# Head copies behind each weight chunk, and index sums in one block: a two-model transformer kernel on one core

## What is computed

```python
h = rmsnorm(x, norm_g)
proj = h @ w_in                     # 1024 -> queries, keys, values, gates
ya = moba_attention(rope(a_q), rope(a_k), a_v)            # 6 heads
# sparse attention "dsa": scores of 4 index heads choose 64 keys for each query
logit = einsum(iq, ik)
idx_score = sum over 4 index heads of relu(logit) * iw
idx_score = where(key <= query, idx_score, -inf)
sel = top_k(idx_score, 64)
yb = attention(rope(b_q), rope(b_k), b_v) over the chosen keys   # 6 heads
yc = dilated_mixture(rope(c_q), rope(c_k), c_v)            # 12 heads
merged = sum of sigmoid gates * (y @ w_branch);  x + merged @ w_out
```

## Time and profile before

| | before |
|---|---|
| median of 3 executions | 2262.8 us |
| the profiled execution, its own time | 2264.01 us |
| its span | 2262.2 us |
| its mean granted TensorE clock | 0.996 of full |
| PE busy | 2205.5 us, 97% |
| POOL, DVE, ACT busy | 1341.6, 1062.3, 837.1 us |
| data moved by DMA | 356.38 MB, mean 158 GB/s |

### The profile page before, as it was taken

The page is one execution under the profiler, slowest core; times in us unless marked ns, Lnnn a source line. Parts: engine busy times, 40 slices in busy tenths (PEclk is TensorE's granted clock), DMA queues, the critical chain, the costliest instruction groups (busy, mean ns, idle before and its releaser), DMA issues.

```text
span 2262.2 us, 38755 instructions
## 1 busy us (share of the span) xinstructions
PE 2205.5 (97%) x13484; PEld 1966.9 (87%) x13484; DVE 1062.3 (47%) x2066; ACT 837.1 (37%) x1294; POOL 1341.6 (59%) x704
## 2 busy tenths in 40 slices
PE   8889998899999999999999999999999999999999
PEld 8889998889988888888888888888888988999999
DVE  7664466654665544267555422655522511233323
ACT  5355553554532222244222222422222413665444
POOL 6664786648765554423555444555544644558997
PEclk9999999999999999999999999999999999999999
DMA  8942468624455543312555432555533423325555
GB/s 300 250 152 101 149 242 253 200 86 141 149 214 194 201 160 92 105 62 104 212 185 190 143 108 89 201 197 187 196 89 96 163 103 102 104 77 178 188 181 158
DMA packets 111378, 356.38 MB, mean 158 GB/s; under 512 B 12200, under 2 KB 20904, under 8 KB 110896
## 3 DMA queue, kind: packets, MB, share of 16 engines
q1 hardware_dynamic: 111280, 355.07, 47.1%
HBM read 347.40 MB, written 1.05 MB: 154 GB/s over the span
## 4 chain that ended last, share of the span: by engine, by line
PE 80%; POOL 6%; DVE 6%; issue 4%; DMA 2%; ACT 1%; SPq 1%; POOLq 0%; DVEq 0%; ACTq 0%
PE ps L2086 21%; PE ps L2087 21%; PE ps L2088 21%; POOL w_low L1161 5%; PE ps L2135 2%; PE ps L2136 2%; PE ps L2137 2%; DMA raw<-in_wv_dram 1%; PE ps L2591 1%; PE ps L2257 1%; PE ps L2225 1%; DVE ps L1406 1%; PE ps L2098 1%; DVE idx L1528 1%; PE ps L2290 1%
## 5 line engine op out<-in xcount | busy, mean ns | idle before, releaser
L1161 POOL TENSOR_TENSOR w_low<-raw,w_high 128x1024 fp32r<-128x1024 f32 (+3 forms) x542 | 1200.3, 2224 | 662.4 <-ACT w_high L624 661.6
L624 ACT ACTIVATE w_high<-raw 128x1024 fp32r<-128x1024 f32 (+3 forms) x544 | 537.0, 989 | 1084.8 <-PE ps L2088 844.1
L2086 PE MATMUL ps<-h_high,w_high 128*128 128x256 f32 (+2 forms) x2408 | 804.3, 334 | 21.7 <-POOL w_low L1161 12.5
L2087 PE MATMUL ps<-h_low,w_high 128*128 128x256 f32 (+2 forms) x2408 | 794.5, 330 | 0.0
L2088 PE MATMUL ps<-h_high,w_low 128*128 128x256 f32 (+2 forms) x2408 | 794.4, 330 | 0.0
L2086 PEld LDWEIGHTS ps<-h_high,w_high 128*128 128x128 f32 x2408 | 455.9, 189 | 68.1 <-issue 16.9
L2088 PEld LDWEIGHTS ps<-h_high,w_low 128*128 128x128 f32 x2408 | 457.0, 190 | 42.3
L2087 PEld LDWEIGHTS ps<-h_low,w_high 128*128 128x128 f32 x2408 | 456.2, 189 | 42.8
L2086 PE MATMUL ps<-act_high,w_high 128*128 128x256 f32 (+1 forms) x1058 | 345.6, 327 | 1.5 <-DVE act_low L2022 1.5
L2087 PE MATMUL ps<-act_low,w_high 128*128 128x256 f32 (+1 forms) x1058 | 344.7, 326 | 0.0
L2088 PE MATMUL ps<-act_high,w_low 128*128 128x256 f32 (+1 forms) x1058 | 344.7, 326 | 0.0
(11 more groups left out here) (251 smaller groups left out, 2236.2 us busy)
## 6 DMA issues: line engine op xcount, KB each, us to landing
raw<-in_w_dram SPq DMA_DIRECT2D x216, 512.0 KB, 3.3
raw<-in_wu_dram SPq DMA_DIRECT2D x176, 512.0 KB, 4.1
ada<-in_ada_dram SPq DMA_DIRECT2D x144, 512.0 KB, 3.3
raw<-in_wd_dram SPq DMA_DIRECT2D x64, 384.0 KB, 3.1
raw<-in_wd_dram SPq DMA_DIRECT2D x64, 320.0 KB, 2.9
raw<-in_wv_dram SPq DMA_DIRECT2D x24, 408.0 KB, 5.1
heads<-rot SPq DMA_DIRECT2D x16, 256.0 KB, 9.3
ada<-in_cond_dram SPq DMA_DIRECT2D x6, 512.0 KB, 5.2
```

The lines of the kernel that those rows point to most:

```text
L624: e.activation(wh[:, c % RING, at_:at_ + w], raw[:, c % RING, 0:w], ACT.Copy).then_inc(hi_done, 1)
L1161: e.tensor_tensor(wl[:, c % RING, at_:at_ + w], raw[:, c % RING, 0:w], wh[:, c % RING, at_:at_ + w].bitcast(F32), ALU.subtract).then_inc(l ...
L2086: e.matmul(ps[:, bank, to:to + n], wh[:, j, w], hi, start=(first and t == tiles[0]), stop=False)
L2087: e.matmul(ps[:, bank, to:to + n], wh[:, j, w], low, start=False, stop=False)
```

## The change

**Heads.** The copies are cut smaller: each group of four heads has 8 copies of 64 KB (32 rows, 2 tiles, 256 columns), two for each quarter of the partitions. Behind the load of chunk c (counted through qk and vn) two of them are issued, for group (c-13) // 4 and quarter (c-13) % 4, from chunk 13 on; they wait until the four chunks of their own group are rotated. The last two and the four of 32 KB come behind the last vn chunk's load, ahead of the first mix chunk's. A layer has 52 copies instead of 20, with the same bytes. PE waits for all of them at the same place.

**Index sums.** `index_step` becomes `index_scores(qt)`, all five operations in a row, called right ahead of the first top-k round of each half: in unit 0 (behind the maxima of units 0 and 1 and the gates 0 to 2) and in unit 8 (behind the maxima of 8 and 9 and the division of unit 7). The last sum has a semaphore of its own, `idx_summed`.

```diff
-            def heads_of(d0, g, n, parts):
-                e.wait_ge(emptied_d, 4 + d0 + RING * (g + n))
+            def heads_of(d0, g, parts=range(4)):
+                e.wait_ge(emptied_d, 4 + d0 + RING * g + RING)
                 for jq in parts:
                     for r in range(2):
                         dst = 64 * (jq % 2) + 32 * r
-                        e.dma_start(head_tiles[dst:dst + 32, 2 * g:2 * g + 2 * n, jq // 2, :],
-                                    rot_tiles[32 * jq:32 * jq + 32, 2 * g:2 * g + 2 * n, r, :]).then_inc(heads_in, 16)
+                        e.dma_start(head_tiles[dst:dst + 32, bass.ds(2 * g, 2), jq // 2, :],
+                                    rot_tiles[32 * jq:32 * jq + 32, bass.ds(2 * g, 2), r, :]).then_inc(heads_in, 16)
+
+            def heads_behind(d0, c):
+                c -= 3 * RING + 1
+                if c >= 0:
+                    heads_of(d0, c // RING, (c % RING,))
...
                         if j % 2 and i > 1:
                             ada_row(r0 + 2 * (i - 1) + j // 2, j // 2)
-                        if i == QK // RING - 1:
-                            heads_of(d0, 0, 4, (j,))
+                        heads_behind(d0, RING * i + j)
...
                         if i == 0 and j % 2:
                             ada_row(r0 + ADA_L - 2 + j // 2, j // 2)
-                        if i == 2 and j < 2:
-                            heads_of(d0, 4, 2, (2 * j, 2 * j + 1))
-                        if i == 2 and j == 2:
-                            for jq, half in ((2, 1), (3, 0)):
...
+                        heads_behind(d0, QK + RING * i + j)
+                heads_behind(d0, QK + VN)
+                for jq, half in ((2, 1), (3, 0)):
+                    for r in range(2):
+                        dst = 64 * half + 32 * r
+                        e.dma_start(heads[dst:dst + 32, NPOS // 2, :],
+                                    rot[32 * jq:32 * jq + 32, QK - 2 + r, :]).then_inc(heads_in, 16)
                 load(m1 + VN, 2 * RING, W8, w1_d, w0 + QK)
...
-                def index_step(qt, h):
+                def index_scores(qt):
                     w = P * (qt + 1)
                     acc = idx[:, qt, 0:w]
...
+                    e.wait_ge(relu_done, n_relu())
+                    e.tensor_scalar(acc, relu[qt][:, 0, 0:w], iw[:, qt, 0:1], None, ALU.mult).then_inc(dve_step, 1)
+                    own(1)
+                    for h in range(1, 4):
+                        last = e.scalar_tensor_tensor(out=acc, in0=relu[qt][:, 2 * (h % 2) + h // 2, 0:w], scalar=iw[:, qt, h:h + 1],
+                                                      in1=acc, op0=ALU.mult, op1=ALU.add)
+                        if h < 3:
+                            last.then_inc(dve_step, 1)
+                            own(1)
+                    last.then_inc(idx_summed, 1)
+                    e.wait_ge(idx_summed, n_relu.now)
+                    e.tensor_tensor(idx[:, qt, w - P:w], idx[:, qt, w - P:w], tri, ALU.add).then_inc(dve_step, 1)
+                    own(1)
...
                 n_nsplit(2 * KT)
-                for h in range(5):
-                    index_step(0, h)
                 gate_out(0)
...
                         qt, n = divmod(u, TOPK // 8)
+                        if n == 0:
+                            index_scores(qt)
                         top_round(qt)
-                        if 3 <= u < 8:
-                            index_step(1, u - 3)
...
                 def index_logits():
-                    e.wait_ge(heads_in, 320 * L + 320)
+                    e.wait_ge(heads_in, 832 * L + 832)
```

More of the change, by code:

```diff
@@ L341, in program @@
         relu_done = sem("relu_done")
+        idx_summed = sem("idx_summed")
         scored = sem("scored")
@@ L1518, in _ @@
                 tri = mask[:, 0:P]
-                def index_step(qt, h):
+                def index_scores(qt):
                     w = P * (qt + 1)
                     acc = idx[:, qt, 0:w]
[L1523 to L1531, removed]
-                        e.tensor_tensor(idx[:, qt, w - P:w], idx[:, qt, w - P:w], tri, ALU.add).then_inc(dve_step, 1)
-                        own(1)
+                    e.wait_ge(relu_done, n_relu())
[11 more added lines that the diff above has]
+                    own(1)
                 def top_round(qt):
```

## The result

The changed kernel took 2247.6 us (median of 9 executions, 2245.65 to 2255.2) beside 2261.25 us for the kernel before in the same comparison (9 executions): a ratio of 0.9934, 95% interval 0.992 to 0.9949, that is 11.5 to 18.1 us less. The forecast was 2246 (2236 to 2257), and 16.9 us less.

The account below looks back on a forecast made before the run. PE was taken as the bound, busy 2205.5 of 2262.2 us, so only its idle or lowered-clock time could be won. -19.3 + 6 + 2 - 7.2 + 5 - 5.4 + 2 = -16.9 us gave 2246 us (2236 to 2257).

Parts of the forecast that it names:

- Large copies gone, small ones added: Head copies in qk and vn: PE idle and lowered clock end, -19.3 us; the small copies' DMA load gives back +6.
- The 6 us put down to the DMA engines: Stretch from 45 to 118 us: nearly balanced between DMA and PE, 3.0 us lost a layer, +6 us, between 3 and 16.
- I cost it at nothing beyond the 3.0 above, covered by the ring: SP's queue: the load after each `ada` row comes 1.24 us later, costed at nothing beyond the DMA term's 3.0 a layer.
- My price of a pair: Two 64 KB head copies cost 0.84 us of all DMA engines, so two qk chunks need 6.5 us.
- End of vn: Eight issues, 5.0 us, ahead of the first mix load; PE may wait at the logits: 1.0 a layer, +2 us.
- Half 0: Index sums moved to unit 0: waits on gate and lowered clock end, -7.2 us; stands there give back +5.
- I counted four of five operations as able to stand: Index sums: by the skill's rule on GpSimd and VectorE exclusion, four of the five sums can stand.
- Half 1: Steps leave units 3 to 7, two PE waits a layer end, -5.4 us; unit 8's block gives back +2.
- Sum: Whole kernel: all terms together give -16.9 us, 2264.0 to 2247.1, and 2246 us on the median.
- Sums blocked again: Rival, units 0 and 8: start costs 3.7 us in each layer and unit 8 loses 3 us; 2252 us, chance 0.18.
- DMA-paced: Rival, from chunk 13 on: engines stay full, pairs cost PE 8 us a layer instead of 3; 2256 us, chance 0.16.
- Slower by SP: Rival, SyncE's queue: each pair's 1.24 us of issue delays the next load and reaches PE; 2276 us, chance 0.05.

Follow-up runs that it names:

- heads_only: Changed kernel with its small head copies, but the index sums back in their old single-step places: 2252.2 us, ratio 0.9948 to the kernel before.
- heads_before_ada: Changed kernel with the two head copies behind an odd chunk issued ahead of the `ada` row instead of behind it: 2244.0 us, ratio 0.9918.
- after_again: The changed kernel itself, unaltered, measured once more in a later comparison: 2248.0 us, ratio 0.9937 to the kernel before.
- half1_ahead: Changed kernel with half 1's index sums as single steps, each ahead of its top-k round, and no block in unit 8: 2242.2 us, ratio 0.9909.
- issues_doubled: Changed kernel with each head copy split into two of 32 KB, four behind each chunk, same bytes: 2280.7 us, ratio 1.008.
- spread_before_ada: Changed kernel, half 0 sums over units 0 to 2, rounds in 3 to 18, half 1 steps ahead of rounds, copies ahead of `ada` row: 2237.4 us, 0.9888.
- pairs_128k: Changed kernel with half as many head copies of 128 KB, two behind every second chunk from 13 on: 2252.5 us, ratio 0.9947.
- small_bunched: Changed kernel with its 64 KB copies issued in groups of eight where the large ones stood: 2273.2 us, ratio 1.0027.

## Why the prediction was right, and where a step of it was wrong

- **Large copies gone, small ones added (-19.3 + 6 = -13.3).** Right in sum. "14 to vn" fell by 6.6 and 6.5 us, 13.1 in all, and by 13.0 in heads_only. The PE waits of over 3 us and the clock of 0.54 are gone, as foreseen. Whether the spreading or the end of SP's wait for chunk 15 does it, no run parts.
- **The 6 us put down to the DMA engines: right size, by luck, and the cause wrong at least in part.** The step that failed is "I cost it at nothing beyond the 3.0 above, covered by the ring", said of the load after the `ada` row. Four times the 5.44 us of two chunks with PE never idle are 21.8; the stretch took 24.8, which is my 3.0. But heads_before_ada takes most of it away (22.5) without moving a byte less, and over all profiles the order is worth 1.4 us of the 2.4 between 24.2 and 21.8. So the 1.24 us of SP's issue in front of that load, which I had put at nothing, was a good part of the cost, though not in every layer. My price of a pair, 0.84 us of all engines, was too high: it gave 6.5 us for two chunks, and heads_before_ada ran them in 5.6. I had divided 10.1 us among six copies in a stretch in which the queue was choked, and a share of 1.00 told me only that packets were under way, not that the engines could do no more. The Trainium skill (page "DMA: Bandwidth & Descriptors", section "Bandwidth") states its rule of batching and its 138 GB/s for 64 KB for loads from HBM that GpSimd issues; I had carried them over to copies within SBUF that SyncE issues, and no run here shows that rate for one. The rule did not decide here: 128 KB copies were no better than 64 KB at the same spread, 64 KB in one heap lost 21 us or more, and 32 KB lost most, by SP's issue time.
- **End of vn (+2).** Right size, other place: the logits waited for nothing, but the eight issues made the mix loads late, ACT rounds these ahead of `relu`, and PE waited 0.90 and 1.12 us there (0.66 and 0.57 in after_again), before only 0.23 in layer 0. The code says this order; I had followed PE's queue and not ACT's.
- **Half 0 (-7.2 + 5 = -2.2).** "Vn to unit 2" went from 17.0 to 17.5 and from 19.7 to 17.5 us, -1.6 with the wait on `relu` in it; against heads_only -2.8 and -2.5. The give-back was one stand and 1.46 and 1.34 us of PE, where I had taken 2.5 a layer. The rule of the Trainium skill (page "SBUF — State Buffer", section "SBUF: two separate sides") agrees in every block, up to 2.5 us for the one operation that stands. I counted four of five operations as able to stand. That was a misreading: the mask's addition has two SBUF inputs too, so by the same rule all five can, and half1_ahead shows it (2.53 us).
- **Half 1 (-5.4 + 2 = -3.4).** "Unit 2 to 10" fell by 2.3 and 2.4 us, 4.6 in all. Both terms were too small. The two waits that I counted in each layer were three, with the 1.07 us behind `pick`: 7.5 us instead of 5.4. The block of unit 8 gave back 1.63 and 1.61 us and not 1.0 a layer.
- **Sum.** Up to the br stage of layer 1 the two profiles of the changed kernel are 22.9 and 19.8 us ahead, a little more than my 16.9. In the first of the two some 2 us are TensorE's pace and not the change (last section). The ratio says 14.9 (11.5 to 18.1).
- **The rivals.** Sums blocked again: half true, one stand a block instead of three. DMA-paced, at 8 us a layer: false, the small copies cost about 3. Slower by SP: false for this kernel, but its mechanism is real. issues_doubled shows it past the edge, and heads_before_ada shows a small part of it in the changed kernel.

## What to carry to other kernels

A DMA that is moved can cost its issue time to whatever stands behind it on that queue: put it into a wait that the queue has anyway, ahead of the instruction that waits, not behind. A full DMA share is no proof that the DMA engines are the bound; change the order without changing the bytes, and look whether PE speeds up, in more than one profile. Where a VectorE operation stands until GpSimd's current one ends, its price depends on when it starts within the other engine's rhythm. A step moved by about 1 us won some 2 us here, and the operation behind it could lose as much, as `pick` did in half1_ahead.

## What was not expected of the hardware

TensorE showed two paces at a granted clock of 1.00. PE alone in the last feed-forward block, 40 us of it: before,

```profile
2120.00:2160.00 40.00, 40.00 (x355) 1.00 0.55 190
```

the changed kernel, in the same profile in which the stretch ahead of the block had a lowered clock,

```profile
2060.00:2080.00 20.00, 17.59 (x128) 0.91 0.54 178
...
2120.00:2160.00 40.00, 40.00 (x342) 1.00 0.55 182
```

and the same kernel again, after_again:

```profile
2120.00:2160.00 40.00, 40.00 (x355) 1.00 0.60 196
```

With 342 instead of 355 matmuls in 40 us, never idle, the last 160 us took some 6 us longer. In this block the changed kernel fell into the slower pace in one of its two profiles, heads_only in its one, the ten others did not (issues_doubled has an excess of 3.6 us in the rest that I did not follow). So it is no trait of the change, and 6.2 us are some 40% of the effect. The two paces occur within one execution as well. The kernel before, qk stage of layer 0 and of layer 1, PE's row of one line and the window:

```profile
L2086 PE MATMUL ps<-h_high,w_high x39: 276/276/276, 44.9 to 57.8; 128*128 128x256 f32 x39
L2086 PE MATMUL ps<-h_high,w_high x72: 281/281/281, 324.8 to 349.9; 128*128 128x256 f32 x72
325.00:350.00 25.00, 25.00 (x215) 25.00 (x214) 20.27 (x36) 9.98 (x10) 22.80 (x10) 1.00 0.80 298
```

At 276 ns a matmul two chunks take 5.44 us there, at 281 ns 5.65. The profile "changed" had the quick pace in layer 1, which is some 2 us of its lead; after_again and spread_before_ada had the slow one. In the last block a lowered clock came just before in both slow profiles, but it did too in half1_ahead, pairs_128k, small_bunched and issues_doubled (windows of 5 or 10 us at 0.67 to 0.88 between 2070 and 2120 us), and their pace afterwards was 355. What selects it stays open, as does how many of the unprofiled executions were in it. That is why the cuts, up to a point that the change can reach, were worth more here than the spans.
